# Attention stage: transposes three items behind the scores, copies four behind, finished pairs an item later

## The reference

```python
def mla_attend(q_nope, q_rope, k_nope, k_rope, v):
    s = (jnp.einsum('bqhd,bkhd->bhqk', q_nope, k_nope)
         + jnp.einsum('bqhr,bkr->bhqk', q_rope, k_rope))
    p = jax.nn.softmax(s.astype(jnp.float32) * ATTN_SCALE, axis=-1).astype(v.dtype)
    return jnp.einsum('bhqk,bkhd->bqhd', p, v)
...
attn_l = mla_blocked(qn_l, qr_l, keys..., values...)        # 8 heads, 2 blocks of 128 queries
mix_l = jnp.concatenate([attn_l, pool_out_l], axis=-1) @ mix_out_w[e]
x = x + g1 * mix_l
```

## Time and profile before

| | us |
|---|---|
| median of 3 runs | 1339.19 |
| lowest and highest run | 1339.14, 1340.3 |
| the profiled execution | 1338.04 |
| its span, first to last instruction | 1336.2 |
| PE, DVE, ACT busy in the span | 1305.7, 444.7, 235.5 |

### The profile page before, as it was taken

The page is one execution under the profiler, slowest core; times in us unless marked ns, Lnnn a source line. Parts: engine busy times, 40 slices in busy tenths (PEclk is TensorE's granted clock), DMA queues, the critical chain, the costliest instruction groups (busy, mean ns, idle before and its releaser), DMA issues.

```text
span 1336.2 us, 28388 instructions
## 1 busy us (share of the span) xinstructions
PE 1305.7 (98%) x12612; PEld 679.8 (51%) x12612; DVE 444.7 (33%) x897; ACT 235.5 (18%) x397; POOL 14.6 (1%) x28
## 2 busy tenths in 40 slices
PE   6998999999999999999999999999999999999997
PEld 5855999999997333333333333433333333333333
DVE  2767489999756101120020020112003002011203
ACT  2556444333353000000000000010000000000002
POOL 0210000000000000000000000000000000000000
PEclk9999999999999999999999999999999999999999
DMA  9674278998735879998998999999799899989980
GB/s 393 261 298 167 103 295 338 382 375 335 291 146 202 319 310 376 420 419 347 421 422 353 414 421 376 393 390 421 300 423 419 352 417 421 413 354 420 421 337 34
DMA packets 59063, 457.68 MB, mean 343 GB/s; under 512 B 6688, under 2 KB 6816, under 8 KB 7616
## 3 DMA queue, kind: packets, MB, share of 16 engines
q1 hardware_dynamic: 58944, 455.87, 84.1%
HBM read 454.80 MB, written 1.05 MB: 341 GB/s over the span
## 4 chain that ended last, share of the span: by engine, by line
PE 90%; DVE 5%; DMA 2%; issue 1%; ACT 1%; SPq 0%; DVEq 0%; PEldq 0%; ACTq 0%
PE bank L1844 43%; PE bank L1857 22%; PE bank L1713 6%; PE bank L1515 3%; PE bank L1703 3%; DVE work L987 2%; PE bank L1562 2%; PE bank L1824 1%; PE bank L1437 1%; DVE split L972 1%; PE bank L1477 1%; DMA ring<-in_mixa 1%; DMA ring<-in_ada 1%; PE bank L1814 1%; PE bank L1763 1%
## 5 line engine op out<-in xcount | busy, mean ns | idle before, releaser
L1844 PE MATMUL bank<-ring,work 128*32 128x512 f32 (+1 forms) x6144 | 584.9, 539 | 1.1 <-DVE moe L1374 1.1
L1844 PEld LDWEIGHTS bank<-ring,work 128*32 128x32 f32 x6144 | 198.8, 110 | 377.3 <-issue 344.4
L1857 PE MATMUL bank<-ring,moe 128*32 128x512 f32 x2688 | 294.1, 592 | 0.0
L1374 DVE TENSOR_TENSOR moe<-moe,bank 128x256 f32<-128x256 f32 (+1 forms) x96 | 31.5, 383 | 647.7 <-ACT moe L875 647.7
L1857 PEld LDWEIGHTS bank<-ring,moe 128*32 128x32 f32 x2688 | 87.2, 110 | 197.8 <-issue 196.4
L875 ACT ACTIVATE moe<-bank 128x256 f32<-128x256 f32 (+1 forms) x96 | 27.4, 357 | 795.4 <-PE bank L1844 795.4
L1713 PE MATMUL bank<-split 128*128 128x256 f32 x1056 | 131.0, 284 | 0.3
L1713 PEld LDWEIGHTS bank<-split 128*128 128x128 f32 x1056 | 128.0, 192 | 2.3 <-ACT split L792 1.3
L972 DVE TENSOR_TENSOR split<-ring,split 128x2048 fp32r<-128x2048 f32 x33 | 75.5, 2290 | 11.1 <-PE bank L1515 6.0
L798 ACT ACTIVATE split<-ring 128x2048 fp32r<-128x2048 f32 x32 | 61.3, 1915 | 82.2 <-PE bank L1713 75.1
L987 DVE SCALAR_TENSOR_TENSOR work<-ring,condp,work 128x512 f32<-128x512 f32 x98 | 73.7, 752 | 5.5 <-DMA ring<-in_ada 1.6
(11 more groups left out here) (230 smaller groups left out, 679.9 us busy)
## 6 DMA issues: line engine op xcount, KB each, us to landing
ring<-in_moe SPq DMA_DIRECT2D x336, 1024.0 KB, 12.3
ring<-in_ffn SPq DMA_DIRECT2D x16, 2048.0 KB, 8.8
ring<-in_ada SPq DMA_DIRECT2D x28, 1024.0 KB, 7.2
ring<-in_ada SPq DMA_DIRECT2D x10, 2048.0 KB, 12.4
ring<-in_mixout SPq DMA_DIRECT2D x2, 2048.0 KB, 7.9
ring<-in_fnet SPq DMA_DIRECT2D x2, 2048.0 KB, 9.7
ring<-in_mixa SPq DMA_DIRECT2D x1, 2048.0 KB, 13.0
ring<-in_mixb SPq DMA_DIRECT2D x1, 1664.0 KB, 12.0
```

Of the source, the lines that this page charges most:

```text
L1374: nc.vector.tensor_tensor(gate_e[:, g, 0:n], gate_e[:, g, 0:n], bank[g][:, n:2 * n], ALU.mult).then_inc(e_hidden, 1)
L1844: last = mm(bank[g][c * QUAD:(c + 1) * QUAD, 0:count * P], x_group[:, 4 * half + k, j * CAP + g * QUAD:j * CAP + (g + 1) * QUAD], source[: ...
L1857: last = mm(bank[3 + n][c * QUAD:(c + 1) * QUAD, :], hiddenT[phase % 2][:, g, blk * QUAD:(blk + 1) * QUAD], source[:, j, n * 512:(n + 1) * ...
```

## The change

On PE the transposes stand three items behind the scores instead of two, and each attend one item later (n = 7, 11, 15). On ACT the copies stand four items behind the exponentials instead of three. On DVE `attended` comes at n = 8 and 12, and for the third pair after the last normalisation. The sums, sizes and buffers are the same.

```diff
--- before.py
+++ after.py
@@ -754,8 +754,8 @@
                                      bank[3 + n % 2][:, :].rearrange("p (a b) -> p a b", a=4), ACT.Copy).then_inc(probsT_taken, 1)
 
             for n in range(len(ITEMS)):
-                if n >= 3:
-                    turn_probs(n - 3)
+                if n >= 4:
+                    turn_probs(n - 4)
                 act.wait_ge(max_ready, n + 1)
                 if n >= 4:
                     act.wait_ge(probsT_ready, n - 3)
@@ -768,7 +768,7 @@
                         act.wait_ge(pool_ready, g // 2 + 1)
                         nc.scalar.activation(mixed[0][:, NG + g, :], bank[6 + g // 2][:, (g % 2) * T:(g % 2) * T + T], ACT.Copy,
                                              scale=V("pool_scale")[:, g:g + 1]).then_inc(pool_high, 1)
-            for n in range(len(ITEMS) - 3, len(ITEMS)):
+            for n in range(len(ITEMS) - 4, len(ITEMS)):
                 turn_probs(n)
             mixer_highs("mixout", len(EARLY_MIX))
             unit_wait(act, first_unit["ffn0"])
@@ -1127,8 +1127,8 @@
                                         ALU.mult).then_inc(probs_ready, 1)
 
             for n in range(len(ITEMS)):
-                if n >= 7 and n % 4 == 3:
-                    attended((n - 7) // 4)
+                if n >= 8 and n % 4 == 0:
+                    attended((n - 8) // 4)
                 dve.wait_ge(scores_ready, n + 1)
                 link(nc.vector.tensor_reduce(small[:, 32 + n:33 + n], bank[n % 3][:, :], AX_X, ALU.max))
                 nc.vector.tensor_scalar(small[:, 32 + n:33 + n], small[:, 32 + n:33 + n], -SCALE, None,
@@ -1140,6 +1140,7 @@
                 if n - 1 in EARLY_MIX:
                     mixer_lows("mixout", EARLY_MIX.index(n - 1), EARLY_MIX.index(n - 1) + 1)
             normalised(len(ITEMS) - 1)
+            attended(HEADS // 2 - 2)
             for g in range(NG):
                 dve.wait_ge(pool_high, 2 * (g // 2) + 2)
                 nc.vector.scalar_tensor_tensor(out=mixed[1][:, NG + g, :], in0=bank[6 + g // 2][:, (g % 2) * T:(g % 2) * T + T],
@@ -1644,10 +1645,10 @@
                     pe.wait_ge(exp_ready, n - 2)
                 mm(bank[n % 3][:, :], queries[0:QK, hd, q * P:(q + 1) * P], keys[0:QK, hd, :],
                    start=True, stop=True).then_inc(scores_ready, 1)
-                if n >= 2:
-                    turn(n - 2)
-                if n >= 6 and n % 4 == 2:
-                    attend((n - 6) // 4)
+                if n >= 3:
+                    turn(n - 3)
+                if n >= 7 and n % 4 == 3:
+                    attend((n - 7) // 4)
                 if n == 1:
                     ada_turn(1)
                 if n in ADA_ITEMS:
@@ -1663,7 +1664,7 @@
                                   start=True, stop=True)
                         if g % 2:
                             last.then_inc(pool_ready, 1)
-            for n in range(len(ITEMS) - 2, len(ITEMS)):
+            for n in range(len(ITEMS) - 3, len(ITEMS)):
                 turn(n)
             project("mixout", mixed, MIX_BANKS, 1, 2, 6)
             spread_root(1, 6)
```

## The result

The changed kernel takes 1341.66 us (median of 20 runs, 1340.28 to 1344.78) against 1338.87 (20 runs) for the one before: a ratio of 1.0017, 95% interval 1.0011 to 1.0024. The medians lie 2.8 us apart; the ratio stands for 2.3 us (1.5 to 3.2). So the change made the kernel slower, clear of the scatter. By the ratio this is within the 0.2% (2.7 us) that the prediction called no change, by the medians just over it, and 1341.66 lies inside its range. But the forecast was 0.88: it is too small by 1.4 us by the ratio, by 1.9 us by the medians. The profiled execution ran 1342.9 us.

The account below looks back on a forecast made before the run. No engine is full in the attention stage; the chain through PE's first projection matmul bounds the kernel. Terms -0.66, +1.35 and +0.19 us give +0.88, so a median of 1340.1 us, range 1338.2 to 1342.9.

Parts of the forecast that it names:

- rival 2: Third attend: the 2.7 us wait ahead of it drops PE to its lower clock, 2.8 us more, 1342.9; chance 0.12.
- The path: Whole chain: whatever the attention stage gains or loses before the first projection matmul reaches the end one for one.
- The start: Attention stage up to the ninth scores: fifth scores at 102.22, ninth at 110.72; -0.66 us.
- The middle: Ninth to thirteenth scores: second attend at 118.96 after waiting 2.1 us for the copy of item 7; +1.35 us.
- The end: Thirteenth scores to projection: third attend waits 2.68 us, behind L769's scalings, until 130.69; projection at 134.32; +0.19 us.
- The sum: Attention stage: -0.66, +1.35 and +0.19 us make the projection 0.88 us later; expected median 1340.1 us.
- rival 1: Attention stage: the transposes' waits of 3.7 us go and nothing takes their place, 1335.5 us; chance 0.06.
- rival 3: Loss partly hidden: copy 11 slips ahead of L769's 1.43 us (1338.7), or the DVE-bound stretch swallows the shift (1339.2); chance 0.15.

Follow-up runs that it names:

- the kernel whose projection is 4.3 us earlier: Changed kernel with copies three items behind and the four pool scalings behind all copies: 1334.75 us against 1339.50 for the kernel before, ratio 0.9968.
- The pure shift of 0.76 us: Kernel before with 2 matmuls of no use on PE between the last transposes and the output projection: 1339.77 us beside 1339.50, ratio 1.0004.
- filled: Changed kernel with matmuls of no use in PE's waits ahead of the second and third attend: 1341.33 us (ratio 1.0015), again 1341.05 (1.0014).

## Why the prediction was right or wrong

The number came out inside the range, and the size of the order was right. The mechanism was right in part only: the clock was left out of the sum, and that term was larger than the one forecast. The range held the result because it reached up to rival 2, to which the prediction gave 0.12. By its own sign for rival 2, "a PE row at a longer mean after the third attend", that rival came about. To that extent the number was luck.

**The path.** Right. What the stage loses comes to the end: from the projection's start to the end are 1202.0 to 1204.9 us in 13 of 14 traces, and the kernel whose projection is 4.3 us earlier (129.25) is 4.7 us faster. The pure shift of 0.76 us gave 0.3 (-0.5 to 1.7), which alone would decide nothing.

**The start.** Right: fifth scores at 102.30 (102.22 worked out), ninth at 110.74 (110.72).

**The middle.** Right in its order part: second attend at 118.97 (118.96), wait 1.87 (2.1). It missed that the clock could fall there: 2.96 us for the attend instead of 1.95, in one trace of three.

**The end.** Right in its order part: with the clock held, the third attend is at 130.83 (130.69) and the projection at 134.52 (134.32). The difference to before, 1.0 against 0.88, is the size of the forecast.

**The step that failed** is the one on the clock. The prediction saw the 2.7 us wait, took its effect for a rival with 0.12 and left it out of the sum. In all three traces the clock fell at that very wait, which was 2.93 us long, and at the projection it cost 3.1, 1.2 and 1.7 us; the rival's price of 2.8, from L1531 against L1536, lies in this span, above the mean of 2.0. "No stretch shows less than 1.00" was no evidence: that stage had no wait longer than 1.1 us. The Trainium skill ("TensorE: Matmul & The Clock Gate", "HAM oscillation — how this bites in real kernels") warned that PE loses its clock over waits; these traces agree, with 0.64 as the mean clock of the attend behind such a wait.

**The sum.** Forecast 0.9; measured 2.3 (ratio) to 2.8 (medians). In the three traces the projection is 3.0 us late on average, 1.0 by the order and 2.0 by the clock, and nothing more is lost behind it. The medians of whole runs give the clock 1.1 only (filled against not filled), not clear of the intervals; the scatter between runs leaves this gap open.

**The rivals.** The waits of the transposes did go (rival 1), but new ones took their place. Rival 2 is what happened at the third attend; its time, 1342.9, was 1.2 us too high against the median. The 1.43 us of L769 (rival 3) were real: moving them gave 1.3 at the projection. And that ACT's order alone was the price is shown by the kernel that undoes it: -2.9 us at the projection from the same PE and DVE order.

## What to carry to other kernels

When two engines are decoupled by a longer distance, only those steps should move that the distance is for. In this kernel a copy that feeds the engine again belongs as early as its operand allows, and work that nobody waits for yet (here the scalings) behind it. With the program orders of three engines and a dozen durations from one trace this reordering could be worked out on paper to some 0.3 us at full clock, and it found a version 4.7 us faster. Add to it a price for PE's clock wherever it leaves a wait on PE that is longer than any wait of the kernel before.

## What the runs showed of the hardware that I had not expected

PE's clock fell behind waits of 1.6 to 2.9 us in this stage, in some executions and not in others. Behind a wait of 2.9 to 3.2 us ahead of the third attend it fell in all four traces that have one (three of the changed kernel, one of the kernel with DVE's part undone). Behind the wait of 1.87 or 1.88 us ahead of the second attend it fell in one trace of five. Behind waits of 1.6 to 1.8 us of transposes it fell in two traces (copies three behind, DVE's part alone) and not in two others (DVE's part undone, PE's part alone). No trace shows a fall in this stage where no wait was longer than 1.5 us.

So two executions of one kernel with the same waits can differ: the projection of the changed kernel came 2.2 us late in one trace and 4.1 in another. The mean clocks of single runs show it too: 0.995 to 0.998 in the changed kernel, 0.999 in half of the runs with filled waits. The spread of the times doesn't: it is 4.5 us over 20 runs of the changed kernel, 4.6 over 35 of the kernel before and 5.9 over 12 of the filled one.

The one row that could have told the price beforehand was the slow first matmul group of the program, L1531, after 8 us of idling. That this group ran at the lower clock is inferred from its 634 ns against 379; the granted clock that the trace gives for it, from 8.2 to 14.6 us, reads 1.00.
